# Sample attention of a decoder trunk: whole sequences, whole key pages turned on TensorE, keys and values by GpSimd's indirect transfers

## The reference, cut to what matters

```
fox:  s = q.k / 8 + F_q - F_k          (F: running sum of log forget values)
moba: s = q.k / 8 + t5_bias[bucket(q_pos - k_pos)]
      of the four past blocks of 256 keys, the three with the largest q . mean(k) count
both: p = softmax(s over the past keys that count, and the own 8 rows, causal);  o = p v
```

## Time and profile before

| | us |
|---|---|
| median of 3 runs (lowest, highest) | 875.64 (874.06, 880.31) |
| the profiled execution | 873.11 |
| its span in the trace | 871.3 |
| of that: until sample attention starts | 228.9 |
| sample attention | 257.0 |
| from there to the end | 385.4 |

### The profile page before, as it was taken

How to read it: one execution, slowest core, us unless ns; L and a number is a source line. 1 busy time by engine, 2 the same in 40 slices (tenths; PEclk the granted TensorE clock), 3 DMA queues, 4 the chain that set the end, 5 groups by cost and what they waited for, 6 DMA issues and landing times.

```text
span 871.3 us, 12979 instructions
## 1 busy us (share of the span) xinstructions
PE 629.8 (72%) x4594; PEld 357.7 (41%) x4594; DVE 398.8 (46%) x826; ACT 168.2 (19%) x427; POOL 175.7 (20%) x214
## 2 busy tenths in 40 slices
PE   4699999977466655656666798849777877877830
PEld 2356466534333232323343577635433433433410
DVE  1513012137676677667687624634233233233226
ACT  2111003027421111111120213411111111111114
POOL 2201302430006336335353000211000000000020
PEclk9899999998766667676586898769999899899885
DMA  9996789833268677686657805355999999999933
GB/s 326 406 374 179 276 314 356 317 136 122 63 228 277 230 267 252 213 308 229 205 144 253 325 2 231 121 205 204 418 421 421 418 421 420 419 419 421 411 99 120
DMA packets 70763, 238.99 MB, mean 274 GB/s; under 512 B 8754, under 2 KB 8939, under 8 KB 62404
## 3 DMA queue, kind: packets, MB, share of 16 engines
q1 hardware_dynamic: 48658, 179.32, 52.5%
q0 software_dynamic: 13968, 43.89, 16.2%
q10 hardware_dynamic: 8098, 15.28, 4.9%
HBM read 220.58 MB, written 17.87 MB: 274 GB/s over the span
## 4 chain that ended last, share of the span: by engine, by line
PE 36%; DMA 24%; DVE 22%; another core or an unknown queue 6%; issue 6%; ACT 2%; SPq 1%; POOL 1%; ACTq 0%; DVEq 0%; POOLq 0%
DMA ring<-w 17%; PE ps L1593 8%; PE ps L1902 7%; DVE work L1152 5%; PE ps L1597 5%; PE ps L1815 4%; DMA ring<-w_in 3%; PE ps L1911 2%; DVE p_half L1223 2%; PE ps L1488 2%; PE ps L1697 2%; DVE mx_b L1199 1%; DMA work<-scr_h 1%; DVE work L1214 1%
## 5 line engine op out<-in xcount | busy, mean ns | idle before, releaser
L1902 PE MATMUL ps<-ring,work 128*64 128x256 f32 x1024 | 135.9, 425 | 28.5 <-DMA ring<-w 25.8
L1902 PEld LDWEIGHTS ps<-ring,work 128*64 128x64 f32 x1024 | 82.2, 153 | 73.2 <-issue 45.6
L1697 PE MATMUL ps<-work 128*32 128x256 f32 x512 | 58.5, 608 | 55.7 <-DVE work L1152 55.7
L1388 DVE TENSOR_SCALAR work<-work 128x128 f32<-128x128 f32 x32 | 15.7, 490 | 161.0 <-ACT work L845 161.0
L571 POOL DMA_INDIRECT ring<-cache_moba_v,v_row x64 | 60.5, 946 | 138.4 <-PE ps L1742 114.8
L571 POOL DMA_INDIRECT ring<-cache_fox_v,v_row x64 | 60.9, 951 | 91.1 <-PE ps L1488 38.2
L1593 PE MATMUL ps<-xh,ring 128*128 128x320 f32 x256 | 73.3, 445 | 7.0 <-DMA ring<-w_in 7.0
L1152 DVE STREAM_TRANSPOSE work<-ring 128x2048 f32<-128x2048 f32 x32 | 71.8, 2284 | 0.0
L598 POOL COPY work<-work 128x512 f32 x32 | 19.6, 614 | 229.7 <-PE ps L1902 212.7
L1593 PEld LDWEIGHTS ps<-xh,ring 128*128 128x128 f32 x256 | 49.5, 196 | 29.1 <-DMA ring<-w_in 7.2
L1911 PE MATMUL ps<-ring,work 128*64 128x512 f32 x256 | 60.5, 593 | 0.7 <-ACT work L849 0.4
(11 more groups left out here) (318 smaller groups left out, 834.8 us busy)
## 6 DMA issues: line engine op xcount, KB each, us to landing
ring<-w SPq DMA_DIRECT2D x96, 1024.0 KB, 13.8
ring<-w_ada SPq DMA_DIRECT2D x4, 4096.0 KB
ring<-cache_fox_k SPq DMA_DIRECT2D x64, 256.0 KB
ring<-cache_moba_k SPq DMA_DIRECT2D x64, 256.0 KB
ring<-w_ada SPq DMA_DIRECT2D x4, 2048.0 KB, 13.5
ring<-w_in SPq DMA_DIRECT2D x2, 4096.0 KB
scr_y<-work ACTq DMA_DIRECT2D x64, 128.0 KB, 6.1
ring<-w_in SPq DMA_DIRECT2D x2, 2048.0 KB
```

Of the source, the lines that this page charges most:

```text
L1388: steps = [lambda: ts(s, s, 1.0, None, ALU.add), lambda: nc.vector.reciprocal(s, s), lambda: tt(s, s, a, ALU.mult), lambda: tt(hid[:, par, ...
L1697: last = mm(o.rearrange("p (q n) -> p q n", q=2), q_cur[:, u.g, 2 * h + e, :], ktv[:, :, 2 * h + e, :], start=(e == 0), stop=(e == 1))
L1902: last = mm(o, h_cur[:, par, c, :], w[:, c, f], start=(c == 0), stop=(c == KC - 1))
```

## The change

Sample attention goes by sequences, fox and moba together, written out for p = 0 to 7 on all engines, with no loop:

- A key or value row set is now 4 successive tokens of 2 KB, 8 KB in one piece, for each of 128 partitions: an indirect transfer brings 1 MB (four pages of one cache), two of them a sequence's part of one cache. All go through GpSimd's queue. Keys have slot 0 alone (one half for each group), values slots 1 and 2 in turn.
- `turn_keys`: 64 transposes of 128x128 on TensorE for a sequence, four to a bank of `ps[4]` to `ps[7]`; ScalarE copies the 8 fox banks out (`fox_keys`), VectorE the 8 moba banks (`moba_keys`), into `kt`.
- `pair_scores`: the biases of all queries of a sequence stand in a table (`tab`, set up once by `table_rows` and VectorE). Two matmuls with the selection matrix `pick_b` start the two score banks; 16 matmuls with 32-column weights and 512 columns add q.k, 4 + 1 + 1 more with 64 columns for each group's own rows. Scores lie with queries on partitions, so the maximum and the moba gate (`pair_bias`) are reductions along a row, and the exponential (`pair_exp`) reads the banks and sums as it goes.
- `turn_pair`: 9 transposes of the probabilities; ScalarE copies them out (`pair_turned`).
- `pair_values`: 32 matmuls with 32-column weights and 256 columns (both groups' values at once) and 4 for the own rows. `pair_scaled`, `turn_output`, `pair_output` finish a sequence.
- `repeat_queries`, `unit_query`, `own_scores`, `far_tab` and `own` go; `set_queries` (two copies for each group) and two copies into `k_own` come, those of moba in round 5 of prompt attention. GpSimd clears `q_blk` in two parts.
- `w_out` is loaded into slot 0 after the last key turn; experts 0 and 1 after the last `pair_values`, 2 and 3 after `w_out` has been read. `eplace` is turned round accordingly. The rest of the kernel stays.

```diff
+            def load_rows(cache, dst, p, inc):
+                rows = cache[0].rearrange("r (l t) h d -> (r l) (t h d)", t=4)
                 for q in range(2):
+                    pool.indirect_dma_start(dst[:, 2048 * q:2048 * q + 2048], None, rows,
+                                            bass.IndirectOffsetOnAxis(v_row[:, 2 * p + q:2 * p + q + 1], 0)
+                                            ).then_inc(inc, 16)
+            def load_keys(p):
+                for g in range(2):
+                    if p == 0:
+                        pool.wait_ge(ring_free[0], 4)
+                    else:
+                        pool.wait_ge(S["kt_tp"], 16 * (p - 1) + 8 * (g + 1))
+                    load_rows(cache_k[g], slot[0][:, 4096 * g:4096 * g + 4096], p, k_in[g])
+            def load_values(p):
+                if p < 2:
+                    pool.wait_ge(ring_free[1 + p], 3 - p)
+                else:
+                    pool.wait_ge(S["v_done"], p - 1)
+                for g in range(2):
+                    load_rows(cache_v[g], slot[1 + p % 2][:, 4096 * g:4096 * g + 4096], p, v_in[p % 2])
+            load_keys(0)
+            load_values(0)
+            load_values(1)
+            pool.wait_ge(S["out_moba"], 16 * 6)
+            nc.gpsimd.memset(q_blk[:, 1], 0.0).then_inc(S["q_zero"], 1)
+            load_keys(1)
+            for p in range(2, NB):
+                load_values(p)
+                load_keys(p)
...
+            pick(0)
+            fox_keys(0)
+            for p in range(NB):
+                if p + 1 < NB:
+                    pick(p + 1)
+                    fox_keys(p + 1)
+                pair_exp(p)
+                pair_turned(p)
...
+            moba_keys(0)
+            for p in range(NB):
+                pair_bias(p)
+                if p:
+                    pair_output(p - 1)
+                if p + 1 < NB:
+                    moba_keys(p + 1)
+                pair_sums(p)
+                pair_scaled(p)
+            pair_output(NB - 1)
...
+            def turn_keys(p):
+                for g in range(2):
+                    pe.wait_ge(k_in[g], 16 * 2 * (p + 1))
+                    kd = slot[0][:, 4096 * g:4096 * g + 4096].rearrange("p (q t n) -> p q t n", q=2, t=4)
+                    for k in range(8):
+                        c, q = k // 2, k % 2
+                        if g == 1 and k < 4:
+                            pe.wait_ge(S["kt_fox"], 8 * p + k + 5)
+                        elif k >= 4:
+                            pe.wait_ge(S["kt_moba" if g else "kt_fox"], 8 * p + k - 3)
+                        for t in range(4):
+                            last = tp(ps[4 + k % 4][:, t * P:(t + 1) * P], kd[:, q, t, c * P:(c + 1) * P], ident)
+                        last.then_inc(S["kt_tp"], 1)
...
+            def turn_pair(p):
+                pe.wait_ge(S["p_exp"], p + 1)
+                pe.wait_ge(S["kt_moba"], 8 * min(p + 2, NB))
+                for q in range(2):
+                    for t in range(4):
+                        last = tp(ps[6 + q][:, t * P:(t + 1) * P], p_nat[:, 512 * q + P * t:512 * q + P * t + P], ident)
+                    last.then_inc(S["p_tp"], 1)
+                tp(ps[2][0:NS, P:2 * P], p_nat[:, D:], ident).then_inc(S["p_tp"], 1)
...
+            turn_keys(0)
+            pe.wait_ge(S["cb_done"], 1)
+            for p in range(NB):
+                pair_scores(p)
+                if p:
+                    turn_output(p - 1)
+                if p + 1 < NB:
+                    turn_keys(p + 1)
+                turn_pair(p)
+                pair_values(p)
+            turn_output(NB - 1)
...
+            sp.wait_ge(S["kt_tp"], 16 * NB)
+            sp.dma_start(slot[0].rearrange("p (k e) -> p k e", k=KC),
                          w_out[0].rearrange("(k p) e -> p k e", p=P)).then_inc(S["wo_in"], 16)
+            sp.wait_ge(S["v_done"], NB)
+            load_expert(0, 0, exp_in[0])
+            load_expert(1, 1, exp_in[1])
+            sp.wait_ge(S["wo_read"], 1)
+            load_expert(2, 2, exp_in[2])
+            load_expert(3, 3, exp_in[3])
```

More of the change, by code:

```diff
@@ L331, in trunk_kernel @@
         block = ctx.enter_context(nc.Block())
[L334 to L360, removed]
         PROJ = ([(True, 2, j * P, j) for j in range(8)]
@@ L431, in _ @@
             load_ada(5)
[L432 to L464, removed]
+            sp.wait_ge(S["kt_tp"], 16 * NB)
+            sp.dma_start(slot[0].rearrange("p (k e) -> p k e", k=KC),
+                         w_out[0].rearrange("(k p) e -> p k e", p=P)).then_inc(S["wo_in"], 16)
             def load_expert(e, k, inc):
@@ L704, in _ @@
             proj_round(14)
-            for r in range(2):
-                for e in range(2):
-                    last = repeat_queries(0, r, e)
-            last.then_inc(S["qrep_a"], 1)
+            set_queries(0).then_inc(S["q_set"], 1)
             ada_evac(4)
@@ L787, in _ @@
[L787 to L794 removed]
+                if p == 5:
+                    set_queries(1)
+                    nc.scalar.copy(k_own[:, 0:PC, :], qkT[:, PC:2 * PC, NP:])
+                    nc.scalar.copy(k_own[:, PC:, :], qkT[:, 3 * PC:4 * PC, NP:]).then_inc(S["q_set"], 1)
@@ L1630, in _ @@
             proj_round(19)
-            own_scores()
+            table_rows()
             key_rows(3)
@@ L1788, in _ @@
-            pe.wait_ge(S["pr_out"], 8)
-            pe.wait_ge(S["o_init"], 2)
-            for half in range(2):
-                unit_scores(Unit(0), half)
-            for c in range(2):
-                unit_step(Unit(c), Unit(c + 1), Unit(c - 1) if c else None, None)
-            with pe.Fori(0, 2) as turn:
-                for j in range(6):
-                    u = Unit(2 + j, turn)
-                    unit_step(u, u.step(1), u.step(-1), u.step(-2))
-            for c in range(14, NU):
-                unit_step(Unit(c), Unit(c + 1) if c + 1 < NU else None, Unit(c - 1), Unit(c - 2))
@@ new lines, in pair_scores @@
+            def pair_scores(p):
+                pe.wait_ge(S["pick_set"], p + 1)
+                pk = pick_b[p % 2]
+                mm(ps[2][:, 0:NS], pk, tab[:, D:], start=True, stop=False)
+                mm(ps[2][:, 0:NS], pick_own_b[p % 2], const("own_mask", NS), start=False, stop=False)
+                for q in range(2):
+                    mm(ps[q][:, :], pk, tab[:, 512 * q:512 * q + 512], start=True, stop=False)
+                for g in range(2):
+                    pe.wait_ge(S["kt_moba" if g else "kt_fox"], 8 * p + 8)
+                    for c in range(PC):
+                        mm(ps[2][32 * c:32 * c + 32, 0:NS], q_blk[:, g, p, c, :], k_own[:, PC * g + c, :],
+                           start=False, stop=(g == 1))
+                    for q in range(2):
+                        for c in range(PC):
+                            last = mm(ps[q][32 * c:32 * c + 32, :], q_blk[:, g, p, c, :],
+                                      kt[g][:, c, 512 * q:512 * q + 512], start=False, stop=(g == 1))
+                last.then_inc(S["s_mm"], 1)
@@ new lines, in turn_output @@
+            def turn_output(p):
+                pe.wait_ge(S["o_set"], p + 1)
+                for g in range(2):
+                    last = tp(ps[3][:, 2 * P + g * P:2 * P + (g + 1) * P], o_nat[:, g * P:(g + 1) * P], ident)
+                last.then_inc(S["o_tp"], 1)
+            pe.wait_ge(S["pr_out"], 8)
+            pe.wait_ge(S["pick_set"], 1)
+            pe.wait_ge(S["tab_rows"], 4)
+            mm(ps[2][:, 64:68], pick_b[0], tab_sum, start=True, stop=True).then_inc(S["cb_mm"], 1)
+            pe.wait_ge(S["q_set"], 2)
```

534 lines of the change are left out of this document (183 added, 351 removed).

## The result

| | before | after |
|---|---|---|
| median of 6 runs, us | 875.88 (871.22 to 880.31) | 884.61 (882.51 to 888.09) |
| profiled execution, us; its span | 873.1; 871.3 | 885.28; 883.2 |
| up to the sample attention stage | 228.9 | 219.4 |
| the stage | 257.0 | 278.3 |
| behind it | 385.4 | 385.5 |

The ratio after to before is 1.011, 95% interval 1.007 to 1.015: 1.1% slower, about as much as a measurement of this kernel tells from no change.

A forecast was written before the change was run, and what follows sets the result against it. It took sample attention to be bound by a chain of waits, no resource full. Stage 31.2 + 217.2 + 24.5 = 272.9 against 257.0, +15.9, less 4.5 ahead, gives +11.4: 887.0 us on the median, range 868 to 912.

The forecast's parts named there:

- The loop and its order: Sample attention: freed values slot, 8.39 MB loaded, moba keys turned, turn_pair, pair_values form a closed loop; six loops 217.2 us.
- T: Length of one sequence's loop in sample attention: 36.2 us forecast, against 33.7 for a unit pair before.
- From GpSimd's issue to the Fox turn: Part of the loop in which values, then Fox keys load before TensorE turns them: 18.4 us.
- The start and the rate: Loop's loads: DMA engines start 1.9 us after GpSimd's issue, then move data at 405 GB/s.
- rival 2: Sample attention loads: GpSimd's queue limits data to 340 GB/s, T 39.0 us, total 904 us; chance 0.15.
- From the turn to the next issue: Rest of the loop: key turns and copies, turn_pair, pair_values, until GpSimd issues again: 17.8 us.
- First and last sequence: Ends of the sample attention stage, outside the six loops: 31.2 us for the first, 24.5 for the last.
- Ahead of the stage: Prompt attention: fewer ScalarE query copies save 4.5 us, bounds 2 and 5.
- rival 3: Sample attention: TensorE's clock stays down, T 43 us, total 928 us; held-back TensorE signals offered as possible half; chance 0.08.
- 1, even: Sample attention: faster data rate and clock rising in the fox turn give T 34.2 us, total 875; chance 0.18.
- DMA share 0 for 13 us: Expected profile sign in each 36 us period: DMA share 1 for 20 us and 0 for 13.
- Rival 4, faster: From moba keys' landing to freed slot, 9.7 us instead of 12.3 with copies at 0.43; total 863 us; chance 0.09.

The follow-up runs named there:

- Experiments 1 and 2: Changed kernel with keys issued ahead of values: 804.55 us, ratio 0.917; changed kernel without loading MoBA's values from the third sequence on: 853.9 us.
- experiment 8: Changed kernel with keys issued ahead of values and turn_pair writing the scores' banks instead of the key turn's: 783.24 us, ratio 0.897.
- experiment 6: Kernel before the change, with values loaded in two 1 MB transfers per unit instead of eight of 256 KB: 847.55 us, ratio 0.974.
- experiment 4: Changed kernel with 13 unread matmuls keeping TensorE busy before each key turn from the third on: 881.11 us, ratio 1.011.
- experiment 3: Changed kernel with 26 unread matmuls keeping TensorE busy before each key turn from the third on: 931.03 us, ratio 1.061.
- experiment 5: Changed kernel with GpSimd's key issues waiting until the scores of the sequence before are done: 884.1 us.
- experiment 7: Changed kernel with ScalarE's four query and own-key copies in the prompt's sixth step cut into 24: 894.63 us, ratio 1.019.

## Why the prediction was right, point by point

The mechanism was right, and that the total came so near (884.5 forecast for the profiled execution, 885.28 measured; 887.0 for the median, 884.61 measured) was luck. The six loops took 7.3 us more than forecast (224.5 for 217.2), the last sequence 2.0 us less and the part ahead of the stage 5.0 us less, and these errors cancel.

**The loop and its order: right.** Experiments 1 and 2 show it as the cause, by its removal and by a dose. I forecast T = 36.2; it was 37.4.
- From GpSimd's issue to the Fox turn: 18.4 forecast; 19.5, 19.1, 19.4, 19.4, 18.2, 18.8 measured (19.1 on average), so 0.7 of T's miss of 1.2 us is here. The start and the rate stand. In the period shown the engines start 2.0 us after the issue (forecast 1.9), and 6.29 MB have moved by 342.8, 15.6 us later: 403 GB/s for my 405, and rival 2's 340 falls.

```profile
326.50:342.80 16.30, 5.24 (x53) 1.55 (x51) 4.82 (x17) 0.00 (x0) 6.56 (x7) 0.77 0.95 385
```

(The stretch begins 0.7 us before the engines are in full use.) TensorE starts 1.8 us after that moment, where I had priced a landing at 1.0; MoBA's keys are on their way by then, and whether their data went ahead of the last of the Fox keys or the landing was seen later isn't shown. The Trainium skill's fit (DMA: Bandwidth & Descriptors, Anatomy of one DMA), 2.0 us + bytes / 436 GB/s, gives 16.4 us for these 6.29 MB and 17.4 with the 1.0 until they are seen: the trace doesn't agree, and experiment 8's full engines stay at 412 to 419 GB/s. MoBA's keys did land before TensorE asked for them.
- From the turn to the next issue: 17.8 forecast, 18.3 measured. The clock was at the lower level when the turn began and rose within it, as the earlier trace rows had let me expect, and both turns with the copies took 10.9 to 11.8 us for my 12.1. The tail behind was undersized: I priced turn_pair and pair_values at the full clock, 5.4 us and 0.3 to the issue, and from the last copy to the next issue it was 6.1 us in two of the loops and 7.1 to 7.4 in the four in which they ran cold. A warm and a cold pair_values of the changed kernel:

```profile
357.37 3.66 PE L1629 MATMUL ps<-ring,work 128*32 128x256 f32 x64 [0.22 <-ACT work L720]
...
470.10 4.54 PE L1629 MATMUL ps<-ring,work 128*32 128x256 f32 x64
```

with turn_pair 1.06 or 1.70 before it. A pause of 1.8 us in TensorE's work lay ahead in both.

**First and last sequence.** 31.2 forecast, 31.3 measured (219.36 to 250.68). The last took 22.5, not 24.5: I charged the lower clock with 4.3 us, and turn_pair to the scaling took 7.4 in all for my 9.7. The stage's sum is 31.3 + 224.5 + 22.5 = 278.3, against 272.9 forecast.

**Ahead of the stage: the largest miss.** -4.5 forecast with bounds 2 to 5, -9.5 measured. The copies that went are as I had them: what is left of them takes 1.6 us of ScalarE,

```profile
209.12 0.82 ACT L626 COPY work<-work 64x256 f32<-64x256 f32 x2
...
209.95 0.41 ACT L689 COPY work<-work 128x256 f32<-128x256 f32 x1
...
210.26 0.40 ACT L690 COPY work<-work 128x256 f32<-128x256 f32 x1
```

and from the fourth pair of prompt copies to the stage they gave 5.7. The other 3.8 were there before them. The prompt's first transposes reach ScalarE 4.5 us earlier, and 1.0 of it stood already at ScalarE's first exponential; before, they came after a held wait, 1.9 us after the eighth value issue (195.65 + 0.95), and in the changed kernel the row has four issues and is over by 189.6, before TensorE has anything for ScalarE (first row: before, second row: after):

```profile
198.52 0.86 ACT L723 COPY work<-ps 128x384 f32<-128x384 f32 x2 [3.39 <-remote]
```

```profile
194.06 0.83 ACT L671 COPY work<-ps 128x384 f32<-128x384 f32 x2
```

In experiment 6 these copies, with rows of two issues, also come without a wait, at 193.49. No step of the prediction had a term for the issue rows.

**Behind it**: 385.5 for 385.4.

**What I did not see.** The 4.5 us pieces that the profile gives to "another core or an unknown queue", which I left in rival 3 as a chance, go when GpSimd's rows of issues are short, and about half of each was hold (experiment 6). So the change as a whole is two changes: 1 MB transfers of values alone give 23 us (by the ratio) to 27 (by the medians), and, if the two add up, the rest, the new order of attention with keys behind values, costs 32 to 35 on top of that. My forecast compared 36.2 with 33.7 and never asked what 33.7 was made of.

**The rivals.** 1, even: its condition, a clock up for most of the Fox turn, did not hold. Its price was a little low: the prediction's own terms give 34.4 at 420 GB/s, a rate above its bound of 413, and 34.6 at 413, and the two periods at the full clock in experiment 4 took 34.8 and 34.6. 2 and 3 are refuted: data at 403 and more, and a clock that costs at most 2.7 us a period, not 7. (Rival 2's T is 39.2 by its own terms, not 39.0.) The sign "DMA share 0 for 13 us" was a slip too: 36.2 less 20.7 us of data is 15.5, and the period shown has 15.8, with data from 327.2 to 348.1. By the rule in the Trainium skill (TensorE: Matmul & The Clock Gate, PE-mode transpose) the turn would have stayed at half the clock; here 64 transposes took 9.5 us, which half the clock throughout would have made 13.6, and in experiment 8 the stage, transposes included, ran at 1.00. The trace disagrees. Rival 4, faster: VectorE's copies kept their 0.61 us (eight in 4.88), as I held against it.

## What to carry to other kernels

When one queue feeds a loop, put first in it what is needed first and can start first: a transfer that waits for its slot holds all that is behind it, and here two swapped lines were worth 80 us. Before pricing a change against the present period, find out what that period is made of, above all the pieces whose releaser the profile can't name. Then give the next stage its own PSUM banks, if the only thing it waits for is that another stage's copies have left them.

## What the hardware showed that I had not expected

- Results of TensorE can reach ScalarE and VectorE late while GpSimd issues indirect transfers without a break. In all six rows of eight of the changed kernel's loops and in 11 of the 13 in the kernel before's sample attention, waiters came free 1.1 to 2.0 us after the last issue's end (304.61, 336.66), in experiment 3 with TensorE at the full clock as well. With eight issues the wait was 11.1 us and with six 8.3, for an input that was seen after 5.9 where no issue ran as it was done (experiment 5). Two rows of eight held nothing (428.82 and 440.90 of the kernel before), nor did the six indirect writes of the routing stage, during which ScalarE came free on a matmul at 574.58 and at 576.28:

```profile
575.06 0.90 POOL L537 DMA_INDIRECT scr_h<-work,slotu  x1 [0.30 <-issue]
...
576.27 0.97 POOL L537 DMA_INDIRECT scr_h<-work,slotu  x1 [0.30 <-issue]
576.28 0.59 ACT L772 COPY xh<-ps 128x512 f32<-128x512 f32 x1 [1.12 <-PE ps L1735]
```

  Which mechanism does it isn't known, nor whether other pairs of engines are held: no run here tested that.
- A float32 matmul of 512 columns is two passes of 0.43 us: 26 took 22.5 us.
- In experiment 7 the clock fell to half while TensorE waited 4.7 us (211.9 to 216.6), and TensorE ran at half from 216.6 to 231; the changed kernel waited 1.3 us at that place and stayed at 1.00.
- GpSimd's queue alone, on rows of 8 KB, moved 412 to 419 GB/s at a DMA share of 1 (experiment 8).
